# Scans of a bidirectional RWKV-7 step: keys and values of a sub-chunk stacked on 128 rows

## The reference

```
def step(S, inp):
    r_t, w_t, k_t, v_t, a_t, b_t = inp
    sa = jnp.einsum('bhvk,bhk->bhv', S, a_t)
    S = S * w_t[:, :, None, :] + sa[..., None] * b_t[:, :, None, :] + v_t[..., None] * k_t[:, :, None, :]
    return S, jnp.einsum('bhvk,bhk->bhv', S, r_t)
s_final, y = lax.scan(step, s0, (r, w, k, v, a, b), reverse=reverse)
```

## Time and profile before

| | us |
|---|---|
| median of 3 runs | 2711.31 (2705.48 to 2714.87) |
| the profiled execution | 2712.27 |
| its span, first to last instruction | 2710.5 |

### The profile page before, as it was taken

One profiled execution on the slowest core, in us unless ns is written; L12 is line 12 of the kernel. 1 busy time (PEld: TensorE's weight loads), 2 busy tenths in 40 slices (PEclk: granted clock), 3 DMA queues, 4 the chain that ended last, 5 costly groups with the idle time before them and its releaser, 6 DMA issues.

```text
span 2710.5 us, 71758 instructions
## 1 busy us (share of the span) xinstructions
PE 2518.7 (93%) x30328; PEld 2374.9 (88%) x30328; DVE 1825.8 (67%) x3160; ACT 1108.5 (41%) x2233; POOL 1076.7 (40%) x855
## 2 busy tenths in 40 slices
PE   4999999999999998888888887999799999999998
PEld 3899999999999996667677667999799999999998
DVE  4475675856857564565555546799777679678787
ACT  3434244342443413344444443443453353443534
POOL 1233232332323323233333324656456556565662
PEclk8999999999999999999999998999889999999999
DMA  8333425435244265344454446454223233334231
GB/s 317 105 106 113 147 76 172 129 92 171 72 156 143 72 210 140 109 134 137 139 157 146 129 156 184 131 172 107 63 50 91 78 98 74 79 80 103 68 79 71
DMA packets 282428, 329.03 MB, mean 121 GB/s; under 512 B 76288, under 2 KB 215936, under 8 KB 273664
## 3 DMA queue, kind: packets, MB, share of 16 engines
q1 hardware_dynamic: 274448, 278.30, 33.4%
q0 software_dynamic: 5904, 39.32, 7.0%
q10 hardware_dynamic: 1760, 6.82, 0.6%
HBM read 221.47 MB, written 91.36 MB: 115 GB/s over the span
## 4 chain that ended last, share of the span: by engine, by line
PE 82%; DVE 8%; issue 5%; ACT 2%; DMA 2%; SPq 1%; POOL 0%; DVEq 0%; ACTq 0%; POOLq 0%
PE inv L1000 10%; PE gbank L1000 10%; PE ser L1000 9%; PE su L1000 9%; PE gbank L1491 8%; PE inv L1491 7%; PE ser L1491 7%; PE su L1491 7%; PE ser L1162 5%; PE gbank L1162 3%; PE su L1162 3%; PE inv L1162 2%; PE gbank L1203 1%; DVE a_sum L2399 1%; DMA ring<-in_wblocks 1%
## 5 line engine op out<-in xcount | busy, mean ns | idle before, releaser
L982 POOL TENSOR_TENSOR w_lo<-raw_w,w_hi 128x512 fp32r<-128x512 f32 x264 | 426.4, 1629 | 370.0 <-ACT w_hi L1834 370.0
L882 POOL TENSOR_TENSOR wsp<-ring,wsp 128x1024 fp32r<-128x1024 f32 x67 | 215.0, 3208 | 644.3 <-ACT wsp L1593 644.3
L1834 ACT ACTIVATE w_hi<-raw_w 128x512 fp32r<-128x512 f32 x264 | 165.5, 634 | 262.6 <-PE ser L1491 98.3
L1000 PE MATMUL ser<-xn_hi,wsp 128*128 128x384 f32 x816 | 217.4, 339 | 5.7 <-POOL xn_lo L888 5.7
L1491 PE MATMUL gbank<-a_hi,w_hi 128*128 128x288 f32 x616 | 186.9, 303 | 30.1 <-POOL w_lo L982 18.2
L1000 PE MATMUL gbank<-xn_hi,wsp 128*128 128x384 f32 x800 | 213.2, 340 | 0.2 <-issue 0.2
L930 POOL TENSOR_TENSOR tt<-xt,ttm 128x256 f32<-128x256 f32 x72 | 48.3, 672 | 415.3 <-DVE xt L2217 415.3
L1000 PE MATMUL su<-xn_hi,wsp 128*128 128x384 f32 x800 | 210.5, 338 | 0.8 <-issue 0.8
L1000 PE MATMUL inv<-xn_hi,wsp 128*128 128x384 f32 x800 | 210.6, 338 | 0.0
L1820 ACT ACTIVATE a_hi<-a_sum 128x1152 fp32r<-128x1152 f32 x88 | 103.2, 1174 | 223.5 <-DVE a_sum L2407 78.2
L1491 PE MATMUL gbank<-a_hi,w_lo 128*128 128x288 f32 x616 | 185.5, 301 | 0.0
(11 more groups left out here) (396 smaller groups left out, 7518.7 us busy)
## 6 DMA issues: line engine op xcount, KB each, us to landing
ring<-in_wblocks SPq DMA_DIRECT2D x107, 512.0 KB, 5.3
ub<-op_d SPq DMA_DIRECT2D x144, 256.0 KB, 2.9
raw_w<-in_wquads SPq DMA_DIRECT2D x33, 1024.0 KB, 4.9
raw_w<-in_wquads POOLq DMA_DIRECT2D x22, 1024.0 KB, 9.2
op_d<-ar SPq DMA_DIRECT2D x32, 576.0 KB, 5.4
op_d<-bk SPq DMA_DIRECT2D x32, 576.0 KB, 6.2
raw_w<-in_wquads SPq DMA_DIRECT2D x44, 256.0 KB, 3.7
raw_w<-zsum POOLq DMA_DIRECT2D x11, 1024.0 KB, 13.0
```

Of the source, the lines that this page charges most:

```text
L882: GT(wsp[s % 2][1][:], ring[(N_ADA_RING + s) % RING][:], wsp[s % 2][0][:].bitcast(F32), ALU.subtract).then_inc(S["wsplit_lo"], 1)
L982: GT(w_lo[n % 4][:], src, w_hi[n % 4][:].bitcast(F32), ALU.subtract).then_inc(S["wl_ok"], 1)
L1000: return nc.tensor.matmul(out, lhsT, rhs, start=start, stop=stop)
L1834: A(w_hi[s][:], raw_of(op)[:, m, :].rearrange("p (k c) -> p k c", k=KH), ACT.Copy).then_inc(S["wh_ok"], 1)
```

## The change

In the scans u joins v in one tile: `uv[q]` holds, for each direction and sub-chunk, u on one half of the 128 rows and v on the other. `tok` and `gmat` are laid out so that their rows match. So

- `gram(v, d)` has four matmuls of 64 rows x 128 columns of weights (b and k of a sub-chunk) with 128 columns (a and r) in place of twelve. It yields the same four products.
- `serial_s` and `serial_y` have four matmuls of 128 rows x 64 columns each in place of eight. `serial_s` starts no product ahead of u; it waits for u of each direction on its own.
- `u_out` is two activations, one for each direction, each on 64 partitions and 128 elements, in place of one on 128 partitions.
- The A operand of the inverse is the transposed one, so `left` takes `tc` and `right` takes `xtb`, and `ltc` and `lm` are twice as wide: GpSimd's three operations a unit on them are 128 x 256 in place of 128 x 128.
- `vb` is replaced by `uv`: two DMAs of 64 rows in place of one of 128, so seven DMAs per unit.
- In the projections the four operands of a direction lie in one tile `opd[d]` with runs of 64 elements; `operands` has two instructions where it had one at two places (four more a pair), and the sync queue writes `opd[d]` with one DMA per direction, when its last operand is done.

```diff
-        ar0, bk0, ar1, bk1, kd = ([sb(dense, f"{n}_{d}", [P, T]) for d in range(2)] for n in ("ar0", "bk0", "ar1", "bk1", "kd"))
+        opd = [sb(dense, f"opd_{d}", [P, NC, 8, SC]) for d in range(2)]
+        ar0, ar1, bk0, bk1 = ([opd[d][:, :, slice(*at), :] for d in range(2)] for at in ((0, 8, 4), (1, 8, 4), (2, 8, 5), (3, 8, 3)))
...
-                sp.wait_ge(S["op_ok"], 8 * p + OPERANDS.index(name) + 1)
-                sp.dma_start(op_d[p, int(d), :, :, SLOT_OF[kind], :].rearrange("c p t -> p c t"), a3(plane[:])).then_inc(S[f"so_{kind}{d}"], 16)
+                sp.wait_ge(S["op_ok"], 8 * p + 4 * d + 4)
+                sp.dma_start(op_d[p, d].rearrange("c p x -> p c x"), opd[d][:].rearrange("p c a t -> p c (a t)")).then_inc(S[f"so_op{d}"], 16)
...
-                sp.dma_start(vb[q][:, d, :], v_d[p, chunk(d, j)]).then_inc(u_in[q], 16)
+                for n, b in enumerate(halves_of):
+                    sp.dma_start(uv[q][halves_of[1 - n], d, n, :], v_d[p, chunk(d, j), b, :]).then_inc(u_in[q], 16)
...
-                for h in range(2):
-                    hs = halves_of[h]
-                    for n, b in enumerate(halves_of):
-                        smm(gbank[halves_of[n ^ h], h, 0:SC], u[hs, d, 0, b], u[hs, d, 2, b], True)
-                for h in range(2):
-                    hs = halves_of[h]
-                    for b in halves_of:
-                        smm(gbank[b, h, SC:2 * SC], u[hs, d, 2, b], u[hs, d, 1, b], True)
-                for h in range(2):
-                    hs = halves_of[h]
-                    for b in halves_of:
-                        ins = smm(gbank[b, h, 2 * SC:4 * SC].rearrange("p (a t) -> p a t", t=SC), u[hs, d, 3, b], u[hs, d, 0:2, b], True)
+                for n in range(2):
+                    for h in range(2):
+                        hs = halves_of[h]
+                        ins = smm(gbank[:, h, n * C:(n + 1) * C], u[hs, d, BK_AT[n]:BK_AT[n] + C], u[hs, d, A_AT[n]:A_AT[n] + C], True)
...
-                for x in (1, 0):
-                    if x == 0:
-                        pe.wait_ge(S["u_ok"], 2 * u + k + 1)
-                    for d in range(2):
-                        b = halves_of[side(d, k)]
-                        for h in range(2):
-                            ins = smm(ser[halves_of[h], d, SY_S[k]:SY_S[k] + HD], tok[u % TOKS][b, h, 2 * d + x, :],
-                                      vb[q][b, d, halves_of[h]] if x else up[k][b, h, :], x == 1 and k == 0)
-                        if x == 0:
-                            ins.then_inc(S["s_full"], 1)
+                for d in range(2):
+                    x = side(d, k)
+                    pe.wait_ge(S["u_ok"], 4 * u + 2 * k + d + 1)
+                    for h in range(2):
+                        ins = smm(ser[halves_of[h], d, SY_S[k]:SY_S[k] + HD], tok[u % TOKS][:, d, x, halves_of[h]], uv[q][:, d, x, halves_of[h]], k == 0)
+                    ins.then_inc(S["s_full"], 1)
...
-                for x, part in enumerate((1, 3)):
-                    for d in range(2):
-                        z = side(d, k)
-                        b = halves_of[z]
-                        for h in range(2):
-                            ins = smm(ser[halves_of[h], d, z * SC:(z + 1) * SC], vb[q][b, d, halves_of[h]] if x else up[k][b, h, :], g[b, d, h, part, :], False)
+                for d in range(2):
+                    z = side(d, k)
+                    for h in range(2):
+                        ins = smm(ser[halves_of[h], d, z * SC:(z + 1) * SC], uv[q][:, d, z, halves_of[h]], g[:, d, h, 2 * z + 1, :], False)
...
-                A(up[k][:], su[:, :, UU[k]:UU[k] + HD], ACT.Copy).then_inc(S["u_ok"], 1)
+                for d in range(2):
+                    x = side(d, k)
+                    b = halves_of[x]
+                    A(uv[u % LOADS][b, d, x, :].rearrange("p (h v) -> p h v", v=HD), su[b, :, UU[k]:UU[k] + HD], ACT.Copy).then_inc(S["u_ok"], 1)
...
-                ch.step(stt(bk0[d][:], bk0[d][:], 1.0, kk[:], add, mul))
+                for n in range(2):
+                    ch.step(stt(bk0[d][:, :, n, :], bk0[d][:, :, n, :], 1.0, a4(kk[:])[:, :, n, :], add, mul))
```

More of the change, by code:

```diff
@@ L413, in flow_step @@
         sb(sc, "under_ltc", [P, 7168])
-        ltc = [sb(sc, f"ltc{q}", [P, 2, HD]) for q in range(3)]
-        lm = [[sb(sc, f"lm{q}{lev}", [P, 2, HD]) for lev in range(FIRST, LEVELS)] for q in range(2)]
+        ltc = [sb(sc, f"ltc{q}", [P, 2, 2, HD]) for q in range(2)]
+        lm = [[sb(sc, f"lm{q}{lev}", [P, 2, 2, HD]) for lev in range(FIRST, LEVELS)] for q in range(2)]
         tc, xtb = (sb(sc, n, [P, LATE, 2, HD]) for n in ("tc", "xtb"))
@@ L528, in flow_step @@
         halves_of = [slice(0, HD), slice(HD, P)]
+        A_AT, R_AT, BK_AT = [[2 * C * n + x for n in range(2)] for x in (0, SC, 2 * SC)]
         def in_flight(s):
@@ L660, in inverse_out @@
                             rows = block_rows(b ^ h, q)[1]
-                            sp.dma_start(x_d[p, :, rows, h, cs], sub_y(p)[part, h, :, :]).then_inc(S["x_out"], 16)
+                            sp.dma_start(x_d[p, :, rows, b, cs], sub_y(p)[part, h, :, :]).then_inc(S["x_out"], 16)
             def unit_half(v, d):
@@ L1115, in diagonal @@
                                 for b in halves_of:
-                                    x = slice(c * C + b.start, c * C + b.stop)
-                                    last = mm(o[h][b, at], bk0[d][hs, x], ar0[d][hs, x], True, True)
+                                    n = b.start // HD
+                                    last = mm(o[h][b, at], bk0[d][hs, c, n, :], ar0[d][hs, c, n, :], True, True)
                                 if (i, d) == (G - 1, 1):
@@ L1244, in right @@
                     to = slice(RIGHT + x * HD, RIGHT + (x + 1) * HD)
-                    for h in range(2):
-                        for i in range(2):
-                            b = halves_of[h]
-                            ins = smm(inv[halves_of[i], h, to], tc[b, x, i, :], p1[b, i, x, :], True)
+                    for i in range(2):
+                        for b in halves_of:
+                            ins = smm(inv[b, i, to], p1[b, i, x, :], xtb[b, x, i, :], True)
                 ins.then_inc(S["dt_full"], 1)
@@ L1649, in _ @@
                 for kind in "wa":
-                    if p:
+                    if p and kind == "w":
                         for d in range(2):
-                            act.wait_ge(S[f"so_{'ar0' if kind == 'w' else 'bk0'}{d}"], 16 * p)
+                            act.wait_ge(S[f"so_op{d}"], 16 * p)
                     for name, cg in LOW_RANK:
@@ L2594, in constants @@
         s, t = i[:, None], i[None, :]
-        for x, m in enumerate((s > t, s <= t, s < t, s <= t) if d == 0 else (s < t, s >= t, s > t, s >= t)):
+        for x, m in enumerate((s < t, s <= t) * 2 if d == 0 else (s > t, s >= t) * 2):
             k[:, K_GM + (4 * d + x) * SC:K_GM + (4 * d + x + 1) * SC] = blocks(m)
```

112 lines of the change are left out of this document (56 added, 56 removed).

## The result

| | before | after | after, profiled again (`control`) |
|---|---|---|---|
| median | 2717.6 us (10 runs) | 2727.9 us (10 runs) | 2729.1 us (10 runs; before beside it 2714.5) |
| ratio to before, 95% interval | | 1.0049 (1.0031 to 1.0067) | 1.0056 (1.0035 to 1.0076) |
| profiled execution | 2712.3 us, span 2710.5 | 2739.7 us, span 2737.9 | span 2726.8 us |
| first unit's transposes at | 1020.7 us | 1040.2 us | 1035.5 us |
| from there to the last unit's | 602.2 us | 616.0 us | 608.9 us |

The change costs 0.5%. Two stages lose: the projections, of which I expected +3 us and which take 15 to 19 more, and the scans, of which I expected -44 and which take 7 to 14 more.

The account below looks back on a forecast made before the run. TensorE was taken as the bound, 93% busy and running dry of instructions once a packet in the scans. -97 + 5 + 48 + 3 = -41 us against 2712.3 gave 2671, so 2670 for the median; range 2632 to 2706.

Parts of the forecast that it names:

- Part 1: Scans: fewer instructions on TensorE, so nearly all instruction-packet stalls go; 97 us less, of which 5 are kept.
- Part 2: Scans: nine more changes of matmul shape a unit on TensorE, 0.16 us each, net 0.66 a unit; +48 us.
- Part 3: Scans: two activations make u of the second direction 0.18 us later, taken as covered; state's own delay under 0.1.
- the 0.41: Scans: about how much later `gram` of the second direction was to start in a unit, in us.
- Part 4: Scans: GpSimd's three wider operations add 0.63 us a unit, covered by 0.7 before `left` needs them.
- Part 5: Projections and loads: VectorE's added instructions +2 us, loads at the start of the scans +1; together +3, from 0 to +8.
- (b): Rival: a third of the stalls stay, or 64 x 128 shape changes cost more; +30, so 2700 us; chance 0.13.
- (c): Rival: stalls don't depend on how fast instructions are used up; +24, or 2735 us; chance 0.12 together with another rival.

Follow-up runs that it names:

- q64: The changed kernel with each `gram` product cut into two of 64 x 64 and the streamed columns cut in two as well; 1.0069 of before, 2739.4 us.
- scan2: The changed kernel with ystate, sy0 and `serial_y` of the second half ahead of `serial_s` of the same unit; 0.9935 of before, 2702.8 us.
- ystate: The changed kernel with `y_state` of the first half moved ahead of `serial_s`, to fill the wait for u; 1.0009 of before, 2714.5 us.
- quarters: The changed kernel with each `gram` product cut into two of 64 x 64 with the same 128 streamed columns; 0.9985 of before, 2717.0 us.
- burst: The kernel before, with all eight operand writes held back until the pair's last operand is done; 1.0058 of before, 2727.8 us.
- le: The changed kernel with loads and early together; 0.9996 of before, 2714.7 us.
- loads: The changed kernel with the second direction's operand write issued behind the next two weight loads; 1.0051 of before, 2726.6 us.
- early: The changed kernel with the next pair's first state made earlier on VectorE, ahead of the wait for the pair's last product; 1.0058 of before, 2724.4 us.
- all3: The changed kernel with scan2, quarters, early and loads together; 0.9904 of before, 2681.7 us.
- all5: The kernel of all3 without sy0, the move of the first half's `serial_y`; 0.9903 of before, 2682.0 us.
- sy0: The changed kernel with `serial_y` of the first half moved ahead of `gate` and `spread`; 1.0102 of before, 2748.9 us.
- right4: The changed kernel with the products of `right` written to all four quarters, results wrong, only the time of use; 1.0037 of before, 2721.0 us.
- all3n: The kernel of all3 without loads, the operands' second write again ahead of the weight loads; 0.9931 of before, 2687.7 us.

## Why the forecast was wrong, step by step

**Part 1, the stalls: the mechanism right, the size too large.** Packets in the scans fell to 94 (forecast 92), and "issue" all but left the waits. q64 shows the dependence on the rate that the argument needed. But I priced all 128 packets at 0.76. The waits of before give "issue" 60.6 us in 75 gaps (17.9 + 17.7 + 15.1 + 3.5 + 3.3 + 2.7 + 0.4); with 0.17 for each, that is 73 us, not 97. The chain's 12.4%, from which I took 0.58 a packet, also counts idle time between groups: after still has 4.5% of it (I had forecast under 3%), without one such gap. The forecast took 92 of them back, 97 less the 5 that it kept; at most 73 were there to take. 19 us of the forecast gain did not exist.

**Part 2, changes of shape: nearly right.** Nine more changes were to cost 0.66 a unit. Of the 1.25 measured, 0.22 is `right` and 0.24 the wait for u, so 0.8 is left; the step from `gram` to the next group (0.65, where 0.44 and 0.16 make 0.60) has a tenth of it. The three changes that scan2 removes against ystate come to 0.15 each, my price was 0.16. That 64 x 128 counts as a shape of its own, for which I had only the Trainium skill ("TensorEngine Tiling (Array Packing)", Available Configurations), is shown by quarters: 0.21 for two changes, 0.16 of it at the first `gram`. Part 2 makes 10 us of the miss.

**Left out: `right`.** The diff changes its loops, and the prediction says nothing of them. Its records are as many and as large as before, so the count of instructions hid it; the rows that it reads and those that it writes would have given 8 bursts of two for 4 of four, 0.23 a unit, by the same rule that I used for `serial_y`. 16 us.

**Part 3, the wait for u: taken at nothing.** I noted that u of the second direction comes later and that "the products with v no longer fill" the wait, and then put it "in the 0.41" of `gram`, a sum that held no wait at all. The first product now stands ahead of u with nothing between: 0.25 in 65 units, 16 us. ystate took it back, in the unit and in the time.

**Part 4, GpSimd: right.** `left` waits for it 0.4 us in all of the scans of after.

**Part 5, the projections: wrong by 12 to 16 us.** The bank of `ch` came 0.27 later a pair, as forecast. "The last of the eight waited for that already" was true and beside the point: what counts is how many bytes stand behind that wait, 2.36 MB instead of 0.59, and who shares the DMA engines then: two weight loads and the instruction packet for the code behind the diagonal products. burst shows it as a cause on its own. With the second write moved, le has 14 us back; loads, without the move of the first state, has none by its time. The Trainium skill ("Runtime: NRT & Kernel Launch", Instruction fetch mechanics) has the cost of a 16 KB boundary as mostly hidden; that holds in the projections but for this place, and in the scans of after, not in those of before nor behind a burst of DMA.

**The rest.** Stalls 19, `right` 16, u 16, shapes 10 and the projections 12 to 16 make 73 to 77; the miss is 55 (forecast -41; +13 to +15 by the ratios). The sum takes every unit as the typical one, 72 x 1.25 = 90 us. Place by place in a pair, the fastest unit of before against an undisturbed one of control, the nine units take 10.2 us more a pair, 82 in all: the first unit 1.5, the one with the modulation 0.8, the next 1.1, the last 0.6, the other five, all of one kind, 1.25 each. That takes back 8. The time behind the scans is 5 us less than before, with 45 us (control 59) at the half clock in it for 70. The remaining 5 to 9 us are open.

Of the rivals, none named `right`, the wait for u or the projections. (b), "gain and cost nearly cancel", was nearest in kind; (c) was near in its number (2735), but by luck: its reason was wrong, since the stalls did go.

## What to carry to other kernels

A merged DMA is not the same transfer: it starts when its last part is ready, and everything behind it on its queue and on the DMA engines, instruction packets among it, moves with it. For small matmuls, count for every group the quarters it uses at a time, also for those whose number and size stay. And look at the product that stands ahead of a wait: where it is merged into the one behind, the wait is bare, and what repaired it here was to move another group of small products into its place (ystate). When a wait is taken away, look for the next one that the same engine ends: early only moved the pause by one group, and the trace gave it a name that hid it.

## What the runs showed of the hardware

An instruction packet that fell into full DMA engines started up to 4.0 us (burst) after the record at which it was due, 1.0 us in before; TensorE then ran dry for up to 3.3 us. In the scans such stalls grow with the rate at which instructions are used up. With the loads of after, a packet in 5.2 us (q64) has some 21 us of them in 620 us, one in 5.8 us (quarters) 3; before, with other loads, has 73 at one in 4.7 us. The rate alone does not fix them: all3 and all5 both have a packet in 5.6 us, and 11.7 and 3.1 us of "issue".

TensorE's granted clock fell from 2.4 to 1.2 GHz for 3 to 20 us behind idle times of 0.8 to 2.2 us at the start of a pair: in seven of seven pairs in sy0 and in loads, six in right4, in four in after, in three in control, which is the same kernel, and in two in quarters. Such a pause alone does not decide it. all3 still has one of 0.8 to 1.7 us in each of the seven pairs (for tc), without a fall, and its scans have a granted clock of 0.99, as those of all3n and all5 have, the other kernels 0.94 to 0.98. What else differs is not shown. A change elsewhere in the unit can thus cost or save more than its own size, and a profile of one execution can be 12 us off the median.
